# Block attention's probabilities turned in 32x32 squares by VectorE and through scratch memory, in place of TensorE transposes

## The reference, cut to what matters

```
s_own = einsum("hqd,hkd->hqk", qc, k_own) - slopes * d_own     # minus infinity where d_own < 0
s_sel = einsum("hqd,hqjkd->hqjk", qc, kg) - slopes * d_sel     # minus infinity where ic >= own
p = softmax(concatenate([s_sel, s_own]))
out = einsum(p_sel, vg) + einsum(p_own, v_own)
```

## Time and the profile before

| | |
|---|---|
| median of the 3 runs shown | 1285.17 us (1284.91 to 1285.43) |
| span of the profiled execution, first to last instruction | 1282.5 us |
| its own time | not listed apart from the runs; they lie 2.4 to 2.9 us above the span |
| granted TensorE clock, mean | 0.999 |
| PE busy | 99% of the span |
| DVE, ACT busy | 57%, 45% |
| the attention's units on PE | from 783 to 860 us of the span |

### The profile page before, as it was taken

One profiled execution on the slowest core, in us unless ns is written; L12 is line 12 of the kernel. 1 busy time (PEld: TensorE's weight loads), 2 busy tenths in 40 slices (PEclk: granted clock), 3 DMA queues, 4 the chain that ended last, 5 costly groups with the idle time before them and its releaser, 6 DMA issues.

```text
span 1282.5 us, 16066 instructions
## 1 busy us (share of the span) xinstructions
PE 1275.4 (99%) x6462; PEld 1071.2 (84%) x6462; DVE 728.4 (57%) x1083; ACT 576.5 (45%) x988; POOL 7.0 (1%) x8
## 2 busy tenths in 40 slices
PE   9999999999999999999999999999999999999998
PEld 9877898898889888888888898778898888888886
DVE  5767678475576555555533489777653433433333
ACT  5577644245446444444522364576432422322222
POOL 0000001000000000000000000000000000000000
PEclk9999999999999999999999999999999999999999
DMA  8421245322234333333433142123243233333311
GB/s 257 142 78 66 99 132 157 138 54 79 82 99 132 99 99 99 99 99 99 148 99 99 33 152 92 57 66 115 64 151 93 92 97 97 115 99 99 99 50 66
DMA packets 38145, 131.20 MB, mean 102 GB/s; under 512 B 4372, under 2 KB 5908, under 8 KB 37816
## 3 DMA queue, kind: packets, MB, share of 16 engines
q1 hardware_dynamic: 37640, 129.79, 32.3%
q10 hardware_dynamic: 432, 0.39, 0.1%
HBM read 128.07 MB, written 2.10 MB: 101 GB/s over the span
## 4 chain that ended last, share of the span: by engine, by line
PE 99%; DMA 0%; DVE 0%; ACT 0%; issue 0%; DVEq 0%
PE bank L1283 18%; PE bank L1284 18%; PE bank L1285 18%; PE bank L1424 5%; PE bank L1425 5%; PE bank L1428 5%; PE bank L1429 5%; PE bank L1426 5%; PE bank L1427 5%; PE bank L1503 1%; PE bank L1580 1%; PE bank L1566 1%; PE bank L1366 1%; PE bank L1355 1%; PE bank L1525 1%; PE bank L1405 1%
## 5 line engine op out<-in xcount | busy, mean ns | idle before, releaser
L1283 PE MATMUL bank<-xh,whi 128*128 128x512 f32 (+1 forms) x1136 | 414.7, 365 | 0.0
L1285 PE MATMUL bank<-xh,wlo 128*128 128x512 f32 (+1 forms) x1136 | 409.9, 361 | 0.0
L1284 PE MATMUL bank<-xl,whi 128*128 128x512 f32 (+1 forms) x1136 | 409.9, 361 | 0.0
L2176 DVE TENSOR_TENSOR wlo<-stage,whi 128x1024 fp32r<-128x1024 f32 (+1 forms) x222 | 267.5, 1211 | 226.3 <-ACT whi L1699 226.1
L1699 ACT CAST whi<-stage 128x1024 fp32r<-128x1024 f32 (+1 forms) x222 | 228.5, 1036 | 198.1 <-PE bank L1429 157.1
L1283 PEld LDWEIGHTS bank<-xh,whi 128*128 128x128 f32 x1136 | 214.4, 189 | 37.6 <-issue 5.5
L1285 PEld LDWEIGHTS bank<-xh,wlo 128*128 128x128 f32 x1136 | 214.4, 189 | 32.8
L1284 PEld LDWEIGHTS bank<-xl,whi 128*128 128x128 f32 x1136 | 214.5, 189 | 31.7 <-issue 0.2
L1424 PE MATMUL bank<-whi,xh 128*128 128x512 f32 x281 | 110.3, 393 | 0.1
L1425 PE MATMUL bank<-whi,xh 128*128 128x512 f32 x281 | 109.4, 389 | 0.0
L1429 PE MATMUL bank<-whi,xl 128*128 128x512 f32 x281 | 109.4, 389 | 0.0
(11 more groups left out here) (341 smaller groups left out, 1413.0 us busy)
## 6 DMA issues: line engine op xcount, KB each, us to landing
stage<-in_W_m SPq DMA_DIRECT2D x64, 512.0 KB, 3.6
stage<-in_W_up SPq DMA_DIRECT2D x44, 512.0 KB, 3.6
stage<-in_W_down SPq DMA_DIRECT2D x22, 512.0 KB, 3.6
stage<-in_W_in_a SPq DMA_DIRECT2D x19, 512.0 KB, 4.1
stage<-in_W_out SPq DMA_DIRECT2D x16, 512.0 KB, 3.7
stage<-in_W_in_b SPq DMA_DIRECT2D x10, 512.0 KB, 3.6
stage<-in_W_kv_k SPq DMA_DIRECT2D x8, 512.0 KB, 3.3
stage<-in_W_kv_v SPq DMA_DIRECT2D x8, 512.0 KB, 4.1
```

Source lines behind the costliest of these rows:

```text
L1283: e.matmul(b[:, cols], hi[:, k, :], xh[:, k, cols], start=(k == 0), stop=False)
L1284: e.matmul(b[:, cols], hi[:, k, :], xl[:, k, cols], start=False, stop=False)
L1285: last = e.matmul(b[:, cols], lo[:, k, :], xh[:, k, cols], start=False, stop=(k == 7))
L2176: e.tensor_tensor(wlo[:, plan.place[i], c], stage[:, i % NSTAGE, c], whi[:, plan.place[i], c].bitcast(F32), ALU.subtract).then_inc(S["w_lo"])
```

## The change

The transposes on PE and their copies on ACT are taken out. In their place, for each unit: DVE transposes the unit's probabilities in 32x32 squares (one instruction, reading every fourth column, writing into `mb_blocks`, which is `gb[:, 1, :]`); SP stores `mb_blocks` to a scratch tensor in device memory, waits for that, and loads it back in another order into `PTm`; `mb_pv` on PE waits for this load and reads its columns as four runs of 32. In the plan `mb_turn` stands one slot earlier than PE's did, and `mb_pv` of units 0 to 6 mostly one slot later, in a slot of its own. `Lm` is packed, and its buffer is free once DVE has transposed it. The row load "pm" waits for the last store.

```
 MOBA_UNITS = [(p, i) for p in range(2) for i in (3, 2, 1, 0)]
-MOBA_BANKS = [2 if i > 1 else 1 for _, i in MOBA_UNITS]
...
-        tap(3)
-        yield
-
-        self.mb_turn(0)
+        tap(1)
+        self.step("mb_turn", 0)
+        tap(2)
+        yield
+
         self.step("mb_norm", 1)
         self.mb_score(2)
         tap(2)
         yield
-        tap(3)
+        tap(1)
+        self.step("mb_turn", 1)
+        tap(2)
         yield
         self.step("mb_norm", 2)
-        self.mb_turn(1)
-        self.mb_pv(0)
         self.mb_score(3)
         tap(2)
         yield
-        tap(4)
+        self.mb_pv(0)
+        tap(1)
+        self.step("mb_turn", 2)
+        tap(2)
         yield
 
         self.step("mb_norm", 3)
-        self.mb_turn(2)
-        self.mb_pv(1)
         self.mb_score(4)
         tap(2)
         yield
+        self.mb_pv(1)
+        tap(1)
+        self.step("mb_turn", 3)
         self.step("mb_norm", 4)
-        tap(1)
-        yield
-        self.mb_turn(3)
-        self.mb_pv(2)
+        yield
         self.mb_score(5)
         tap(2)
-        yield
-        self.mb_pv(3)
+        self.step("mb_turn", 4)
+        yield
+        self.mb_pv(2)
         tap(1)
         self.step("mb_norm", 5)
         yield
 
         self.lru_gates(0)
-        self.mb_turn(4)
         self.mb_score(6)
-        tap(2)
-        yield
+        tap(1)
+        self.step("mb_turn", 5)
+        tap(1)
+        yield
+        self.mb_pv(3)
         tap(3)
         yield
         self.step("mb_norm", 6)
-        self.mb_turn(5)
         self.mb_pv(4)
         self.mb_score(7)
         tap(3)
         yield
-        tap(3)
+        tap(1)
+        self.step("mb_turn", 6)
+        tap(2)
         yield
 
         self.mb_pv(5)
         self.step("mb_norm", 7)
-        self.mb_turn(6)
         self.lru_gates(1)
         tap(3)
         yield
-        tap(4)
-        yield
-        self.mb_pv(6)
-        self.mb_turn(7)
+        tap(1)
+        self.step("mb_turn", 7)
+        tap(3)
+        yield
         self.step("lru_a")
         tap(4)
         yield
+        self.mb_pv(6)
         tap(60)
...
+        yield
         self.mb_pv(7)
-        yield
         self.cf_mean()
...
+        moba = [nc.dram_tensor(f"moba{u}", (128, 256 * (i + 1)), F32, kind="Internal").ap() for u, (_, i) in enumerate(units)]
...
-                q.wait_ge(S["mb_pt"], sum(MOBA_BANKS[:u + 1]))
+                q.wait_ge(mb_turned[u % 2], 16 * (u // 2 + 1))
                 q.wait_ge(S["v2_out"], 2)
+                PT = PTm[u % 2][:, 0:256 * (i + 1)].rearrange("p (b k c) -> p k b c", b=4, c=32)
...
+            def mb_turn(u):
+
+                m = 2 * units[u][1] + 2
+                q.wait_ge(S["mb_p"], u + 1)
+                if u:
+                    q.wait_ge(S["mb_out"], 16 * u)
+                e.transpose(mb_blocks[:, 0:128 * m].rearrange("p (r k a) -> p r k a", r=4, k=m),
+                            Lm[u % 3][:, 0:128 * m].rearrange("p (k a r) -> p r k a", r=4, k=m)).then_inc(S["mb_tr"])
...
+            def mb_turn(u):
+                w = 256 * (units[u][1] + 1)
+                q.wait_ge(S["mb_tr"], u + 1)
+                e.dma_start(moba[u], mb_blocks[:, 0:w]).then_inc(S["mb_out"], 16)
+                q.wait_ge(S["mb_out"], 16 * u + 16)
+                if u >= 2:
+                    q.wait_ge(S["mb_o_full"], u - 1)
+                e.dma_start(PTm[u % 2][:, 0:w].rearrange("p (b c) -> p b c", b=4),
+                            moba[u].rearrange("(b a) (r c) -> (a r) b c", b=4, r=4)).then_inc(mb_turned[u % 2], 16)
```

More of the change, by code:

```diff
@@ L780, in mb_score @@
         self.step("mb_score", u)
[L782 to L787, removed]
     def mb_pv(self, u):
@@ L891, in beside_mixer_two @@
         yield
+        tap(1)
+        self.step("mb_turn", 7)
+        tap(3)
+        yield
+        self.step("lru_a")
         tap(4)
@@ L894, in beside_mixer_two @@
         self.mb_pv(6)
-        self.mb_turn(7)
-        self.step("lru_a")
-        tap(4)
-        yield
         tap(60)
@@ L1073 @@
     + ["ld_w0", "ld_xf", "w0_lo", "ld_xr", "ld_c", "ld_masks", "ld_bias", "ld_mem", "ld_rows",
-       "ld_mix2", "stored"]
+       "ld_mix2", "mb_out", "mb_in0", "mb_in1", "stored"]
     + ["mm", "tile_done", "vt_full", "half", "gt_full", "swa_s_full", "swa_t_full", "swa_o_full", "gc_full", "ml_m_full", "ml_s_full", "ml_h_full",
        "ml_t_full", "tr_full", "xa_s_full", "xa_t_full", "xa_o_full", "cf_m_full", "cf_v_full", "mb_s_full",
-       "mb_t_full", "mb_o_full", "lru_full"]
+       "mb_o_full", "lru_full"]
     + ["w_hi", "x_hi", "f_hi", "a_own", "a_out", "gate_e", "gate_x", "gate_h", "swa_e", "swa_p", "swa_pt", "swa_y", "qk_y",
@@ L1082 @@
        "up_g", "rms_sd", "cf_first", "cf_g", "cf_sq", "cf_ln", "cf_ex", "cf_th", "qk2_out", "mb_e", "mb_p",
-       "mb_pt", "v2_out", "lru_y", "lru_g", "lru_th", "lru_e", "lru_sqa", "lru_gg", "sc_c", "lru_u", "sc_first", "m1_r", "pn_sq", "x_sq",
+       "v2_out", "lru_y", "lru_g", "lru_th", "lru_e", "lru_sqa", "lru_gg", "sc_c", "lru_u", "sc_first", "m1_r", "pn_sq", "x_sq",
        "lru_rt"]
@@ L1088 @@
        "ln_z", "ln_x", "xa_m", "xa_p", "lam_m", "lam", "hb", "ln_sum", "mg", "up_pad", "up_c", "up_t", "up_h", "eps6", "xn",
-       "cf_z", "cf_taps", "cf_s", "cf_y", "mb_logit", "mb_m", "mb_r", "mb_y", "lru_c", "lru_i", "lru_m",
+       "cf_z", "cf_taps", "cf_s", "cf_y", "mb_logit", "mb_m", "mb_r", "mb_tr", "mb_y", "lru_c", "lru_i", "lru_m",
        "lru_h", "sc_p", "sc_y", "m1_h", "pn_w", "pn_x", "r2", "last"]
@@ L1190, in build_program @@
         yT = tiles(reg(32, 4096), 8)
-        Lm = [tiles(reg(48, 1024), 2), tiles(reg(52, 1024), 2), tiles(gb[:, 0, :], 2)]
-        PTm = [tiles(reg(56 + 4 * i, 1024), 2) for i in range(2)]
+        Lm = [reg(48, 1024), reg(52, 1024), gb[:, 0, :]]
+        PTm = [reg(56 + 4 * i, 1024) for i in range(2)]
+        mb_blocks = gb[:, 1, :]
+        mb_turned = [S["mb_in0"], S["mb_in1"]]
         cz = [reg(64, 542, 542 * i) for i in range(2)]
@@ L1640, in mb_score @@
                 last.then_inc(S["mb_s_full"])
[L1642 to L1652, removed]
             def mb_pv(u):
@@ L1663, in mb_pv @@
                         h = 2 * p + z
-                        last = e.matmul(b[rows64(z), tok(i)], av[:, j, 64 * h:64 * h + 64], PTm[u % 2][:, z, tok(j)],
+                        last = e.matmul(b[rows64(z), tok(i)], av[:, j, 64 * h:64 * h + 64], PT[:, z * (i + 1) + j, :, :],
                                         start=(j == 0), stop=(j == i))
@@ L1683, in _ @@
                         ml_turn=ml_turn, xa_score=xa_score, xa_turn=xa_turn, xa_pv=xa_pv, cf_mean=cf_mean,
-                        cf_var=cf_var, mb_score=mb_score, mb_turn=mb_turn, mb_pv=mb_pv, lru_gate=lru_gate)
+                        cf_var=cf_var, mb_score=mb_score, mb_pv=mb_pv, lru_gate=lru_gate)
             for name, *a in plan.steps:
@@ L2031, in mb_score @@
                 for z in range(2):
-                    Lq = Lm[u % 3][:, z, 0:w]
+                    Lq = Lm[u % 3][:, z * w:z * w + w]
                     e.activation(Lq, Lq, ACT.Exp, bias=mu(u, 0)[:, z:z + 1], accum_out=mu(u, 1)[:, z:z + 1]
@@ L2152, in _ @@
                         cf_var=cf_var, cf_exp=cf_exp, cf_gate=cf_gate, in2_a=in2_a, in2_v=in2_v,
-                        mb_score=mb_score, mb_norm=mb_norm, mb_turn=mb_turn, lru_in=lru_in, lru_gate=lru_gate,
+                        mb_score=mb_score, mb_norm=mb_norm, lru_in=lru_in, lru_gate=lru_gate,
                         lru_a=lru_a, lru_b=lru_b, lru_gelu=lru_gelu, sc_c=sc_c, sc_conv=sc_conv,
@@ L2586, in mb_score @@
                 w = 128 * (i + 1)
-                Lq = Lm[u % 3][:, :, 0:w]
+                Lq = tiles(Lm[u % 3][:, 0:2 * w], 2)
                 q.wait_ge(S["ld_mix2"], 64)
                 if u >= 3:
-                    q.wait_ge(S["mb_t_full"], sum(MOBA_BANKS[:u - 2]))
+                    q.wait_ge(S["mb_tr"], u - 2)
                 q.wait_ge(S["mb_s_full"], u + 1)
@@ L2710, in _ @@
                         last_norm=last_norm, cf_in=cf_in, cf_tap=cf_tap, cf_parts=cf_parts, cf_mean=cf_mean, cf_scale=cf_scale,
-                        cf_out=cf_out, mb_score=mb_score, mb_norm=mb_norm, mb_pv=mb_pv, lru_in=lru_in, lru_a=lru_a,
+                        cf_out=cf_out, mb_score=mb_score, mb_norm=mb_norm, mb_turn=mb_turn, mb_pv=mb_pv, lru_in=lru_in, lru_a=lru_a,
                         lru_b=lru_b, lru_scan=lru_scan, sc_x=sc_x, sc_conv=sc_conv, sc_b=sc_b, post_norm=post_norm,
@@ L2782, in rows @@
                 elif which == "pm":
-                    q.wait_ge(S["mb_t_full"], sum(MOBA_BANKS))
+                    q.wait_ge(S["mb_out"], 128)
                     e.dma_start(*row(0, "post_mix_g_2")).then_inc(S["ld_rows"], 16)
@@ L2810, in _ @@
                 x_load(k)
-            mine = dict(begin=begin, bias_load=bias_load, split=split, x_in=x_in, consts=consts, mem_load=mem_load, x_again=x_again, rows=rows, mix2_loads=mix2_loads, store=store)
```

(1 more changed line is left out.)

## The result

| | before | after |
|---|---|---|
| median, 21 runs each | 1285.08 us (1284.49 to 1286.16) | 1287.14 us (1286.51 to 1287.66) |
| span of the profiled execution | 1282.5 us | 1285.8 us |
| mean granted clock | 0.999 | 0.998 |

The changed kernel is slower by 2.06 us: ratio 1.0015, 95% interval 1.0009 to 1.0021. The forecast was 1.1 us faster. The time lies inside the outer range of 1282.4 to 1291.0, 0.3 us above the forecast's own (1283.0 to 1286.8), and on the other side of the kernel before.

What follows compares the result with a forecast made beforehand. The prediction took PE, busy for 99% of the span, as the bound. Terms: -3.8 us on PE, +2.7 of waiting, so -1.1: from 1285.17 to 1284.1 us, own range 1283.0 to 1286.8.

Steps and rivals of the forecast that it cites:

- outer range: Whole kernel: 1282.4 to 1291.0 us, from the no-waits case to somewhat above the doubled squares.
- the price of the DVE transpose: DVE's eight new transposes: priced like a plain pass over as many columns, 5.65 us in all, both ends kept.
- the prediction's own sign of being wrong: Transposes of 2 us or more, PE waiting for scores or at cf_mean, loads over 5 us, or ACT casts awaiting weights.
- the first rival: DVE's transposes cost twice a pass because of the four-column read step: slower, 1289.3 us, chance 0.33.
- the 0.5 us that was free: DVE idle time left over, of 3.35 us waiting for scores 3 and 4, after transposes 0 to 3.
- PE would like `mb_pv(4)`: When PE would reach mb_pv(4) unhindered: 833.9 us, 3.1 earlier than before; data ready at 834.7, so 0.8 us wait.
- its own mark of 0.2%: Whole kernel: about 0.2%, 2.6 us, is what a measurement can tell from no change.
- PE's own gain: On PE: 40 transposes less, 4.8 us, minus 1.0 for more groups and dearer entries, so 3.8 us.
- The strided read of `mb_pv`: On PE, mb_pv reading columns in four runs of 32: taken as free, bounds nothing to near 3 us.
- The two places of the waits: PE waits 0.8 us at mb_pv(4) and 1.9 us at mb_pv(5), because DVE runs late there.
- Stores and loads: SP's way through memory: 512 KB stored in 2.6 us, loaded in 3.6, 6.3 with hand-overs from transpose to mb_pv.
- Is the 1.1 us kept?: Behind the stage, at cf_mean and out2's second slice: at most 0.4 + 2.4 = 2.8 us can be kept; 1.1 stays.

Runs made afterwards that it cites:

- e1: Changed kernel with DVE reading each 32x32 square from adjacent columns instead of every fourth (key order then wrong): 1283.55 us, ratio 0.9991.
- e4: Changed kernel with no turning at all: mb_pv reads untransposed probabilities from five Lm buffers, not the reference's output: 1281.76 us, ratio 0.9975.
- e6: Changed kernel plus 14 matmuls with overwritten results on PE ahead of the wait of mb_pv(4): 1287.87 us, ratio 1.0019.
- e10: Changed kernel plus 14 overwritten matmuls ahead of mb_pv(4)'s wait and nine ahead of mb_pv(5)'s: 1286.66 us, ratio 1.0011.
- e8: e5 with mb_pv(4) and mb_pv(5) one slot later each, output the reference's: 1282.61 us, ratio 0.998.
- e3: Changed kernel without the way through memory: DVE writes squares straight into PTm, mb_pv waits for DVE, not the reference's output: 1287.77 us, ratio 1.0022.
- e9: Changed kernel, still reading every fourth column, with mb_pv(4) and mb_pv(5) one slot later each: 1287.03 us, ratio 1.0014.
- e5: Changed kernel with squares read from adjacent columns and key order mended by four loads of 32 partitions per unit: 1283.97 us, ratio 0.999.
- e7: Changed kernel with ten taps of the convolution's second half left out on DVE, transposes still 2.0 us: 1283.28 us, ratio 0.9984.
- e2: Changed kernel with squares read from every second column, 8 bytes apart (key order then wrong): 1283.91 us, one execution.

## Why the prediction was wrong, step by step

**The step that failed** is the price of the DVE transpose: "I price the transpose so: 1.13, 0.85, 0.57 and 0.28, in all 5.65 us ... I take the plain pass, the nearer row". Measured are 2.03, 1.55, 1.10 and 0.63 us, then 2.01, 1.61, 1.11 and 0.64, 10.7 in all; with the 0.1 us by which a successor starts early, some 10. That is the prediction's own sign of being wrong, transposes of 2 us or more. The step itself was in view, every fourth column, 16 bytes, and stood as the first rival with 0.33; it had been weighed by the nearest row instead of by what set this read apart from every row. e1 shows that the operation is priced like a plain pass, and that the step alone makes the difference.

**How it came to the end.** Up to transpose 5 the six instructions took 8.93 us where I had 4.81; less 0.1 each for the overlap and the 0.5 us that was free, that is 3.0 later. In us from the first `mb_score` (forecast and kernel before minus 782.96):

| | forecast | measured |
|---|---|---|
| transpose 4 ends | 45.4 | 47.52 |
| PE would like `mb_pv(4)` | 50.9 | 51.18 |
| `mb_pv(4)` starts | 51.7 | 54.16 |
| transpose 5 ends | 54.9 | 57.70 |
| `mb_pv(5)` starts | 60.8 | 63.50 |

The forecast's error at `mb_pv(5)` is 2.7 us and stays to the end: from there to `out2` before took 36.39 us and after 35.85, a gain of 0.54 where 0.7 was forecast. 2.7 + 0.16 on a forecast of -1.1 is the measured +1.76.

**The rival** of the squares at twice a pass had the right place and direction. At the measured 1.7 times it decides, by its own point of 1.6, for slower. Its 1289.3 was too high with the factor, and since its extra waits at scores and `out2` did not arise in the changed kernel. The forecast's words "this counts as no change" fit the result, 0.15% against its own mark of 0.2%, but by luck: a gain of 1.1 us was forecast and a loss of 2.06 came, both smaller than the mark of 2.6 us.

**What held.** PE's own gain: 3.8 us in the ledger, 3.2 by the times of e4 and 3.54 by its stage. The strided read of `mb_pv` is free: 16 matmuls take 1.09 us, as before. `mb_pv(0)` to `(3)` have no wait. The two places of the waits, and at the plain price about their sizes (e1: 0.28 us for 0.8 and 1.78 for 1.9). Stores and loads.

**What was missed.** First, a long wait can lower PE's clock; in the changed kernel that cost nothing, by e6 and e10, since PE would have waited at `mb_pv(5)` till the same point. Second, "Is the 1.1 us kept?" limited the gain to 2.8 us by ACT and `out2`; e4's gain of 3.5 us still stands at the second slice of `out2`, because DVE ends `x_from` there at 96.27 us, 5.0 earlier than before. Where DVE turns the squares as well, even by the cheap read, that place does bind: e8 starts the slice only 2.6 us earlier than the kernel before, held by DVE. Third, the dear squares set a second limit behind the first. DVE's first half of what `cf_mean` needs is ready 79.73 us into the stage after, and at 79.78, 79.71, 79.69 and 79.70 in e3, e6, e9 and e10, whatever PE waits for or at which clock it runs. Before, `cf_mean` started at 79.46. The same holds at the second slice of `out2`, with more weight: its `x_from` is ready at 102.9 to 103.1 us in the changed kernel and in e3, e6, e9 and e10, and before, PE started the slice at 101.67. So with this read and DVE's list as it is, another place for `mb_pv` leaves the kernel at least 1.2 us slower at that slice; e9 tried one and came to 1.3.

**Left open.** Why the clock falls behind a wait of 1.86 us (e6) and in one execution 1.78 (e1), and not behind 1.93 (e9). The length of the wait alone doesn't decide it.

## What to carry to other kernels

Price an operation by the access pattern that it has here: when a read's step has no row in the trace, its ends deserve as much weight as the nearest row, and a run with that step alone changed would tell. When work moves to an engine that is 84% busy, follow that engine to each later place where the bounding engine needs it; removing one wait shows the next, and only less work on that engine (e1, e5, e7) moves them all. And pair the two repairs: the cheap read alone (e5) gave 3.4 us against the change, the late slots alone 0.3, both together 4.8, each kernel against its own runs of the one before.

## What the runs showed of the hardware

- VectorE's 32x32 transpose of float32: 1.24 us for 1024 columns, 0.44 for 256, at a read step of 4 or 8 bytes (e1, e2); 2.03 and 0.63 at 16 bytes (after). Transposing itself costs no more than a plain pass (1.22 us).
- TensorE's granted clock fell to its lower level behind waits of 2.98 us (after), 3.37 (e3), 1.86 (e6) and in one profiled execution 1.78 (e1); it held behind 1.93 (e9), 1.67 (e2), 1.50 (e7) and 1.35 (e5). The slow stretch cost 1.6 us (e3 against e9) to 1.7 (after, e1, e6).
- A way through device memory and back, 512 KB, takes 2.6 + 3.9 us, 384 KB 2.3 + 3.5, 256 KB 2.0 + 2.9 and 128 KB still 2.6 + 2.2: a quarter of the bytes takes three quarters of the time.
